# A gate matrix from bfloat16 one-hots: each token's product in three bfloat16 parts, in place of one fp32 product

## The chip, the cores and the metric

The kernel runs on one NeuronCore of one Trainium2 chip. The metric is device time in microseconds, the median of several executions. One further execution was taken with the hardware profiler; all rows below come from it.

## What is computed

The reference is one inference step of a one-layer decoder: mLSTM and retention heads, then a PEER mixer (product-key experts). Only the mixer's dense path matters here. For each token it picks 128 pairs (8 heads of 16) of expert and gate:

```python
top_s, top_pos = lax.top_k(cand_s, PEER_TOPK)          # per head: 16 of 256 candidates
e_idx = jnp.take_along_axis(cand_i, top_pos, axis=-1)  # expert = i1 * 128 + i2, of 16384
gate = jax.nn.softmax(top_s, axis=-1)
a = jax.nn.gelu(jnp.einsum('thkd,td->thk', u_tab[eb], xb).astype(jnp.float32), approximate=False)
return jnp.einsum('thk,thkd->td', (gb * a).astype(v_tab.dtype), v_tab[eb])
```

For 768 of the 1024 prompt tokens the kernel takes all 16384 experts, with a gate of zero where an expert wasn't picked. It therefore needs, for every token, the 128 x 128 matrix of gates, element (i2, i1) being the sum of the gates of the picks with that expert.

## The kernel before

The kernel is written in stages, each a block in which the engines run their own programs and meet by semaphores. `up_phase` holds four: the top-k stage, the decode stage, the gate stage and a stage that gathers rows for the other 256 tokens. In all four PE also works through the 128 units `e` of the dense up projection: a tile of `peer_u` is loaded (`u_load`), split into a high part by ScalarE (`u_high`) and a low part by DVE (`u_low`, L1070), and multiplied with the normalised tokens in two halves of 384 tokens (`u_unit`, 24 products of 384 columns each, L1081 to L1083). ScalarE applies the gelu (L1090) and SP stores it.

The decode stage (L1286 to L1396) turns the top-k results into three numbers for each pick: i1, i2 and the gate. PE transposes them, ScalarE writes them to `e3T` (L1349): 128 picks on the partitions, 3 x 776 values along each (768 dense tokens and 8 sample tokens). DVE's last operations there make `e_tok` and `gate_tok` for the 256 other tokens (L1394, L1395) and one `u_low` for each of nine token tiles.

The gate stage (L1399 to L1489) goes over the 768 dense tokens in 96 steps of STEP = 8. In each step DVE makes three tensors of 8 x 128 elements in fp32, by comparing `iota` (0 to 127) with a column of `e3T`: `raw` (where is i2; L1484), `one1[:, b]` (where is i1; L1485) and `one2[:, b]` = `raw` times the gate (L1487). `b` alternates, so there are two buffers. DVE waits for the step two before to leave PE (`step_done`) and, ahead of `raw`, for its own `one2` of the step before (`hot2`). PE waits for `hot1` and `hot2` and does one product for each token: `one2[:, b, k, :]` as the loaded operand, `one1[:, b, k, :]` as the moving one (L1438). The sum over the 128 picks is the token's gate matrix. Four tokens fill a PSUM bank; ScalarE copies each bank into `gbuf` (L1460). After every second step PE does one `u_unit`, after every fourth DVE does one `u_low`. 8 steps fill half of `gbuf`, which SP stores in one transfer of 4 MB (L1421), in its queue ahead of the next `u_load`. The stage after it reads `e3T` again, for the 8 sample tokens (L1601, L1643).

Of the kernel before, what the change touches and what calls it, by code (L numbers as in the profile page):

```python
# [13 lines left out]
BF16 = mybir.dt.bfloat16  # L14
I32 = mybir.dt.int32
ALU = mybir.AluOpType
# [3 lines left out]
P = 128  # L20
# [4 lines left out]
NS = 8  # L25
# [5 lines left out]
PH, NK, TOPK = 8, 128, 16  # L31
GROUPS = [range(0, 4), range(4, NC), range(NC, NT)]
SUB = 64
DENSE = 768
TG = DENSE // P
GT = NC - TG
NG = GT * P
NU = NG + NS
# [5 lines left out]
STEP = 8  # L44
# [992 lines left out]
def up_phase(nc, A, own, sb, ps, sem, ident, hn, x2_dram, hs_dram, g_dram, a_dram, ys, yt, idx, wt):  # L1037
# [4 lines left out]
    uh, ul = (sb(own, "u_" + x, [P, 2, ND, P], F32R) for x in ("hi", "lo"))  # L1042
    av = sb(own, "act_tile", [P, 2, DENSE])
    iota = sb(own, "iota", [P, NK])
    e3T = sb(own, "e3T", [P, 3, DENSE + NS])
    e_tok = sb(own, "e_tok", [P, GT, 2, NK])
    gate_tok = sb(own, "gate_tok", [P, NG])
    pu = [ps(own, f"u_p{g}") for g in range(2)]
    u_in, a_out = ([sem(f"{x}{i}") for i in range(2)] for x in ("u_in", "a_out"))
    uhi_done, ulo_done, up_done, gelu_done, iota_in = (  # L1050
# [2 lines left out]
    def u_load(sp, e, s, first=False):  # L1053
        if not first:
            sp.wait_ge(ulo_done, e - 1)
        sp.dma_start(u_raw[:, s], A["peer_ut"][e]).then_inc(u_in[s], 16)
# [11 lines left out]
    def u_low(dve, e, s):  # L1068
        dve.wait_ge(uhi_done, e + 1)
        nc.vector.tensor_tensor(ul[:, s], u_raw[:, s], uh[:, s].bitcast(F32), ALU.subtract).then_inc(ulo_done, 1)  # L1070
# [22 lines left out]
    with ExitStack() as both:  # L1093
# [192 lines left out]
        with ExitStack() as st, nc.Block() as block:  # L1286
# [6 lines left out]
            se = sb(st, "d_se", [P, NT, PH, TOPK])  # L1293
            sm = sb(st, "d_sum", [P, NT * PH, 2])
            gt = sb(st, "d_gate", [P, NT, K8])
            pt = [ps(st, f"d_t{i}") for i in range(2)]
            diff_done, exp_done, ident_done, oh_done, gt_done, t_done, t_out, chain = (
                sem(n) for n in ("d_diff", "d_exp", "d_ident", "d_oh_done", "d_gtdone", "d_tdone", "d_tout", "d_chain"))
# [2 lines left out]
            PET = TG + 1  # L1301
# [55 lines left out]
            def _(dve):  # L1357
# [16 lines left out]
                for i, t in enumerate(ORDER):  # L1374
# [20 lines left out]
                        v.tensor_copy(gate_tok[:, (t - TG) * NK:(t - TG + 1) * NK], gt[:, t, :])  # L1395
                    u_low(dve, E0 + i + 2, i % 2)  # L1396


    with ExitStack() as st, nc.Block() as block:  # L1399
        HALF = STEP // 2  # L1400
        NSTEP = SUB // STEP
        one1, one2 = (sb(st, f"one{i}", [P, 2, STEP, NK]) for i in (1, 2))
        raw = sb(st, "raw", [P, STEP, NK])
        gbuf = sb(st, "gbuf", [P, 2, NK, SUB])
        pg = [ps(st, f"g_p{i}") for i in range(4)]
        hot1, raw_done, hot2, step_done, bank_full, bank_out = (
            sem(n) for n in ("g_hot1", "g_raw", "g_hot2", "g_step", "g_full", "g_bank_out"))
        saved = [sem(f"g_saved{i}") for i in range(2)]

        @block.sync  # L1410
        def _(sp):
            for s in range(2):
                sp.sem_inc(saved[s], 16)
            with sp.Fori(0, NSUB // 2) as j:
                for s in range(2):
                    for p in range(2):
                        e = G0 + 4 * j + 2 * s + p
                        u_load(sp, e + 2, p)
                        a_store(sp, e, p)
                    sp.wait_ge(bank_out, (2 * NSTEP) * (2 * j + s + 1) + 4)  # L1420
                    sp.dma_start(g_dram[:, :, 2 * j + s].rearrange("q i e t -> i q e t"),  # L1421
                                 gbuf[:, s, :, :].rearrange("i (q e) t -> i q e t", e=2)).then_inc(saved[s], 16)
            for s in range(2):
                sp.wait_ge(saved[s], 16 * (NSUB // 2) + 16)

        @block.tensor
        def _(pe):
            pe.sem_inc(step_done, 2)
            with pe.Fori(0, NSUB // 2) as j:
                for s in range(2):  # L1430
                    for n in range(NSTEP):
                        i, b = (2 * j + s) * NSTEP + n, n % 2
                        pe.wait_ge(hot1, i + 1)
                        pe.wait_ge(hot2, i + 2)
                        for k in range(STEP):
                            if k % HALF == 0:
                                pe.wait_ge(bank_out, 2 * i + k // HALF + 1)
                            last = nc.tensor.matmul(pg[2 * b + k // HALF][:, (k % HALF) * NK:(k % HALF + 1) * NK],  # L1438
                                                    one2[:, b, k, :], one1[:, b, k, :], start=True, stop=True)
                            if k == HALF - 1:  # L1440
                                last.then_inc(bank_full, 1)
                        last.then_inc(step_done, 1)
                        if n % 2:
                            u_unit(pe, G0 + 4 * j + 2 * s + n // 4, n // 4, n // 2 % 2)

        @block.scalar
        def _(act):
            act.sem_inc(bank_out, 4)
            with act.Fori(0, NSUB // 2) as j:
                for s in range(2):  # L1450
                    act.wait_ge(saved[s], 16 * j + 16)
                    for n in range(NSTEP):
                        i, b = (2 * j + s) * NSTEP + n, n % 2
                        for c in range(2):
                            if c == 0:
                                act.wait_ge(bank_full, i + 1)
                            else:
                                act.wait_ge(step_done, i + 3)
                            t = n * STEP + c * HALF
                            nc.scalar.activation(gbuf[:, s, :, t:t + HALF],  # L1460
                                                 pg[2 * b + c][:, :].rearrange("p (t i) -> p i t", t=HALF),
                                                 ACT.Copy).then_inc(bank_out, 1)
                        if n % 2:
                            p, half = n // 4, G0 // 2 + 2 * j + s
                            e = G0 + 4 * j + 2 * s + p
                            u_gelu(act, e, p, n // 2 % 2, half)
                            if n // 2 % 2:
                                u_high(act, e + 2, p, half + 1)

        @block.vector  # L1470
        def _(dve):
            v = nc.vector
            dve.sem_inc(hot2, 1)
            dve.wait_ge(iota_in, 16)
            io = iota[:, :].unsqueeze(1).broadcast_to([P, STEP, NK])
            with dve.Fori(0, NSUB // 2) as j:
                for s in range(2):
                    for n in range(NSTEP):
                        i, b = (2 * j + s) * NSTEP + n, n % 2
                        col = [e3T[:, q, bass.ds(i * STEP, STEP)].unsqueeze(2).broadcast_to([P, STEP, NK])  # L1480
                               for q in range(3)]
                        dve.wait_ge(step_done, i + 1)
                        dve.wait_ge(hot2, i + 1)
                        v.tensor_tensor(raw[:, :, :], io, col[1], ALU.is_equal).then_inc(raw_done, 1)  # L1484
                        v.tensor_tensor(one1[:, b], io, col[0], ALU.is_equal).then_inc(hot1, 1)  # L1485
                        dve.wait_ge(raw_done, i + 1)
                        v.tensor_tensor(one2[:, b], raw[:, :, :], col[2], ALU.mult).then_inc(hot2, 1)  # L1487
                        if n % 4 == 3:
                            u_low(dve, G0 + 4 * j + 2 * s + n // 4 + 1, (n // 4 + 1) % 2)  # L1489


    with ExitStack() as st, nc.Block() as block:
# [3 lines left out]
        idx_f = sb(st, "s_idxf", [P, NU])  # L1496
# [99 lines left out]
        def _(dve):  # L1596
            v = nc.vector
            for t in range(GT):
                v.scalar_tensor_tensor(idx_f[:, t * NK:(t + 1) * NK], e_tok[:, t, 0, :], float(NK), e_tok[:, t, 1, :],
                                       ALU.mult, ALU.add).then_inc(idxf_done, 1)  # L1600
            v.scalar_tensor_tensor(idx_f[:, NG:NU], e3T[:, 0, DENSE:DENSE + NS], float(NK), e3T[:, 1, DENSE:DENSE + NS],  # L1601
                                   ALU.mult, ALU.add).then_inc(idxf_done, 1)
            dve.wait_ge(idxf_done, GT + 1)
            v.tensor_copy(idx[:, :], idx_f[:, :]).then_inc(idx_done, 1)  # L1604
# [25 lines left out]
            for j in range(J0, J1):  # L1630
                u_low(dve, 2 * j + 1, 1)
                if j == J0 + 1:
                    dve.wait_ge(hr_in, 16)
                if j == JG - 1:
                    dve.wait_ge(h_in, 16 * NS)
                rows_of(j, 0)
                if j < J1 - 1:
                    u_low(dve, 2 * j + 2, 0)
                rows_of(j, 1)
                if j == JG:  # L1640
                    dve.wait_ge(act_done, 1)
                    dve.wait_ge(zero_done, 1)
                    v.tensor_tensor(wd[:, :, :].rearrange("p a b -> p (a b)")[:, 0:NS * NS:NS + 1], dots[:, NG:NU],  # L1643
                                    e3T[:, 2, DENSE:DENSE + NS], ALU.mult).then_inc(wd_done, 1)
                    v.tensor_tensor(wt[:, :], dots[:, 0:NG], gate_tok[:, :], ALU.mult).then_inc(wt_done, 1)
                    dve.wait_ge(xt_in, 16)
                    dve.wait_ge(wt_done, 1)
# [355 lines left out]
```

## Time and profile before

| | |
|---|---|
| median of 3 runs | 3474.07 us (3472.54 to 3478.43) |
| the profiled execution's own time | 3476.1 us |
| its span, first to last instruction | 3474.3 us |
| PE, DVE, ScalarE, GpSimd busy | 95%, 73%, 29%, 21% |
| the gate stage in the span | some 1352 to 1738 us |

Times in a row are microseconds from the span's start or durations in microseconds, mean durations nanoseconds. PE is TensorE's matmuls, PEld its weight loads, which overlap them; DVE is VectorE, ACT ScalarE. Matmuls are pipelined: the duration of one is longer than its distance to the next, so rates are read from starts. An fp32 product is two passes, each with its own record.

### The profile page before, as it was taken

How to read it: one execution, taken by the hardware profiler on the slowest of the kernel's cores; microseconds unless marked ns; L12 is line 12 of the kernel's file. 1: busy time of each engine (PE TensorE's matmuls, PEld its weight loads, DVE VectorE, ACT ScalarE, POOL GpSimd, SP SyncE). 2: the span in 40 equal slices, each digit the busy share in tenths (PEclk: the TensorE clock that was granted, in tenths of full speed). 3: DMA queues.
4: the chain of work that ended last, by engine and by line, in shares of the span. 5: the costliest groups of instructions: out<-in, count | busy, mean ns of one | idle time of the engine just before them, and what ended most of it. 6: DMA issues, size and time to landing. Idle time of an engine off the chain costs nothing. (4 is left out here: it accounts for less than half of the span.)

```text
span 3474.3 us, 49500 instructions
## 1 busy us (share of the span) xinstructions
PE 3285.5 (95%) x17444; PEld 2896.5 (83%) x17444; DVE 2526.2 (73%) x5184; ACT 990.4 (29%) x1463; POOL 737.0 (21%) x565
## 2 busy tenths in 40 slices
PE   7989999797999899999989999998999999999998
PEld 5766777587999789999989999996888888888886
DVE  5465555434999968999847777765888887988884
ACT  3212322221111122444412222222333333333332
POOL 0000000000000000000046665554333333433320
PEclk9999999798999999999999999999999999999999
DMA  2111110222111122665599999997999999999983
GB/s 103 38 38 50 62 39 26 80 92 90 50 62 57 48 86 70 209 196 175 184 333 374 371 374 356 355 341 289 403 370 354 352 356 367 379 369 351 355 318 114
DMA packets 323132, 749.92 MB, mean 216 GB/s; under 512 B 22160, under 2 KB 153620, under 8 KB 321864
## 3 DMA queue, kind: packets, MB, share of 16 engines
q1 hardware_dynamic: 243240, 458.48, 36.8%
q0 software_dynamic: 79776, 290.00, 22.3%
q8 instruction: 60, 0.98, 0.1%
q14 instruction: 56, 0.46, 0.0%
HBM read 633.46 MB, written 114.94 MB: 215 GB/s over the span
## 5 line engine op out<-in xcount | busy, mean ns | idle before, releaser
L1081 PE MATMUL u_p<-hn_hi,u_hi 128*128 128x384 f32 x2048 | 705.3, 344 | 37.9 <-DVE u_lo L1070 19.8
L1082 PE MATMUL u_p<-hn_lo,u_hi 128*128 128x384 f32 x2048 | 697.6, 341 | 0.0
L1083 PE MATMUL u_p<-hn_hi,u_lo 128*128 128x384 f32 x2048 | 696.9, 340 | 0.0
L1514 POOL DMA_INDIRECT s_ring<-in_peer_u,row_idx x264 | 331.9, 1257 | 1332.0 <-DVE row_idx L1604 1109.1
L1759 PE MATMUL y_p<-v_hi,w_hi 128*128 128x512 f32 x1536 | 474.3, 390 | 19.5 <-DVE w_lo L1844 18.0
L1716 POOL DMA_INDIRECT y_ring<-in_peer_v,row_idx x240 | 355.9, 1483 | 618.1 <-DVE yt L1853 557.2
L1764 PE MATMUL y_p<-v_hi,w_lo 128*128 128x512 f32 x1536 | 473.4, 389 | 0.0
L1761 PE MATMUL y_p<-v_lo,w_hi 128*128 128x512 f32 x1536 | 473.3, 389 | 0.0
L1785 ACT ACTIVATE v_hi<-v_raw 128x1024 fp32r<-128x1024 f32 x256 | 257.2, 1052 | 664.5 <-PE y_p L1764 653.2
L1840 DVE TENSOR_TENSOR v_lo<-v_raw,v_hi 128x1024 fp32r<-128x1024 f32 x256 | 302.0, 1221 | 171.3 <-ACT v_hi L1785 171.3
L1081 PEld LDWEIGHTS u_p<-hn_hi,u_hi 128*128 128x128 f32 x2048 | 390.0, 190 | 42.6 <-issue 21.9
L1083 PEld LDWEIGHTS u_p<-hn_hi,u_lo 128*128 128x128 f32 x2048 | 389.9, 190 | 0.0
L1082 PEld LDWEIGHTS u_p<-hn_lo,u_hi 128*128 128x128 f32 x2048 | 389.8, 190 | 0.0
L1090 ACT ACTIVATE act_tile<-u_p 128x384 f32<-128x384 f32 x256 | 125.7, 491 | 920.2 <-PE u_p L1083 920.2
L1759 PEld LDWEIGHTS y_p<-v_hi,w_hi 128*128 128x128 f32 x1536 | 288.4, 188 | 81.1 <-DVE v_lo L1840 15.2
L1761 PEld LDWEIGHTS y_p<-v_lo,w_hi 128*128 128x128 f32 x1536 | 288.8, 188 | 60.1
L1764 PEld LDWEIGHTS y_p<-v_hi,w_lo 128*128 128x128 f32 x1536 | 288.6, 188 | 60.0
L1612 DVE CUSTOM_DVE_ANT_0 s_junk<-s_ring,s_hr 128x1024 f32<-128x1024 f32 x256 | 313.3, 1224 | 28.4 <-DVE s_dots L1612 1.0
L1853 DVE SCALAR_TENSOR_TENSOR yt<-y_ring,row_weight,yt 128x1024 f32<-128x1024 f32 x240 | 307.4, 1281 | 22.1 <-DMA y_ring<-in_peer_v,row_idx 5.2
L1070 DVE TENSOR_TENSOR u_lo<-u_raw,u_hi 128x1024 fp32r<-128x1024 f32 x128 | 156.1, 1220 | 185.3 <-ACT u_hi L1066 185.1
L324 PE MATMUL pp<-wp_hi,xn_hi 128*128 128x512 f32 (+1 forms) x576 | 247.5, 430 | 4.1 <-DVE wp_lo L583 3.7
L326 PE MATMUL pp<-wp_hi,xn_lo 128*128 128x512 f32 (+1 forms) x576 | 231.6, 402 | 0.0
(292 smaller groups left out, 4643.7 us busy)
## 6 DMA issues: line engine op xcount, KB each, us to landing
v_raw<-in_peer_v SPq DMA_DIRECT2D x128, 1024.0 KB, 7.0
u_raw<-in_peer_ut SPq DMA_DIRECT2D x128, 512.0 KB, 7.6
act_scratch<-act_tile SPq DMA_DIRECT2D x128, 384.0 KB, 5.4
gate_scratch<-gbuf SPq DMA_DIRECT2D x12, 4096.0 KB, 14.0
a_raw<-act_scratch SPq DMA_DIRECT2D x128, 384.0 KB, 7.6
g_raw<-gate_scratch SPq DMA_DIRECT2D x128, 384.0 KB, 9.2
wp_raw<-in_w_heads SPq DMA_DIRECT2D x64, 256.0 KB, 3.4
wq<-in_w_query SPq DMA_DIRECT2D x8, 1024.0 KB, 5.2
```

The lines of the kernel that those rows point to most:

```text
L1081: mm(b, uh[:, s, k, :], hn_hi[:, k, t], start=(k == 0), stop=False)
L1082: mm(b, uh[:, s, k, :], hn_lo[:, k, t], start=False, stop=False)
L1083: last = mm(b, ul[:, s, k, :], hn_hi[:, k, t], start=False, stop=(k == ND - 1))
L1514: nc.gpsimd.indirect_dma_start(out=ring[:, s, :], out_offset=None, in_=src, in_offset=bass.IndirectOffsetOnAxis(ap=idx[:, column:column + ...
L1612: v.tensor_tensor_reduce(junk[:, :], ring[:, n % RING, :], h, 1.0, 0.0, ALU.mult, ALU.add, dots[:, n:n + 1]).then_inc(dot_done, 1)
L1716: nc.gpsimd.indirect_dma_start(out=ring[:, n % RING, :], out_offset=None, in_=A["peer_v"], in_offset=bass.IndirectOffsetOnAxis(ap=idx[:, N ...
L1759: mm(py[t][i][:, :], wh[:, s, e, tok], vh[:, s, e, i * 512:(i + 1) * 512], start=a, stop=False)
L1761: mm(py[t][i][:, :], wh[:, s, e, tok], vl[:, s, e, i * 512:(i + 1) * 512], start=False, stop=False)
L1764: done = mm(py[t][i][:, :], wl[:, s, e, tok], vh[:, s, e, i * 512:(i + 1) * 512], start=False, stop=z)
L1785: ac(vh[:, s, e, :], v_raw[:, r, e, :], ACT.Copy).then_inc(vhi_done, 1)
L1840: v.tensor_tensor(vl[:, s, e, :], v_raw[:, r, e, :], vh[:, s, e, :].bitcast(F32), ALU.subtract).then_inc(vlo_done, 1)
L1853: v.scalar_tensor_tensor(yt[:, t, :], ring[:, n, :], wt[:, bass.ds(column, 1)], yt[:, t, :], ALU.mult, ALU.add).then_inc(add_done, 1)
```

## The change

The gate matrix is made from bfloat16 tensors. The gate is split into three bfloat16 parts whose sum is the fp32 value exactly. The plain one-hot is now that of i2 (`one2`, the loaded operand); the gate goes into `one1`, which has three parts, and PE adds three products for each token in PSUM. The tensors have the token innermost ([128 keys, 8 tokens] in place of [8 tokens, 128 keys]). `keys`, `iota` spread over 8 tokens in bfloat16, is made once. i1, i2 and the parts (`eb`, `gp`) are made by DVE at the end of the decode stage, behind its last `u_low`; `e3s` keeps the 8 sample tokens' values, and `e3T` lives only in the decode stage.

```diff
+                dve.wait_ge(t_out, PET)
+                ch.mark(v.tensor_copy(e3s[:, :, :], e3T[:, :, DENSE:DENSE + NS]))
+                ch.mark(v.tensor_copy(eb[:, :, :], e3T[:, 0:2, 0:DENSE]))
+                ch.link(v.tensor_copy(gp[:, 0, :], e3T[:, 2, 0:DENSE]))
+                ch.link(v.tensor_tensor(left[:, :], e3T[:, 2, 0:DENSE], gp[:, 0, :], ALU.subtract))
+                ch.link(v.tensor_copy(gp[:, 1, :], left[:, :]))
+                ch.link(v.tensor_tensor(left[:, :], left[:, :], gp[:, 1, :], ALU.subtract))
+                ch.link(v.tensor_copy(gp[:, 2, :], left[:, :]))
...
-        one1, one2 = (sb(st, f"one{i}", [P, 2, STEP, NK]) for i in (1, 2))
-        raw = sb(st, "raw", [P, STEP, NK])
+        one1 = sb(st, "one1", [P, 2, 3, NK, STEP], BF16)
+        one2 = sb(st, "one2", [P, 2, NK, STEP], BF16)
+        raw = sb(st, "raw", [P, NK, STEP], BF16)
+        keys = sb(st, "keys", [P, NK, STEP], BF16)
...
-                        pe.wait_ge(hot1, i + 1)
-                        pe.wait_ge(hot2, i + 2)
+                        pe.wait_ge(hot2, i + 1)
+                        pe.wait_ge(hot1, i + 2)
...
-                            last = nc.tensor.matmul(pg[2 * b + k // HALF][:, (k % HALF) * NK:(k % HALF + 1) * NK],
-                                                    one2[:, b, k, :], one1[:, b, k, :], start=True, stop=True)
+                            for q in range(3):
+                                last = nc.tensor.matmul(pg[2 * b + k // HALF][:, (k % HALF) * NK:(k % HALF + 1) * NK],
+                                                        one2[:, b, :, k], one1[:, b, q, :, k], start=(q == 0),
+                                                        stop=(q == 2))
...
-            io = iota[:, :].unsqueeze(1).broadcast_to([P, STEP, NK])
+            v.tensor_copy(keys[:, :, :], iota[:, :].unsqueeze(2).broadcast_to([P, NK, STEP])).then_inc(keys_done, 1)
+            dve.wait_ge(keys_done, 1)
...
-                        col = [e3T[:, q, bass.ds(i * STEP, STEP)].unsqueeze(2).broadcast_to([P, STEP, NK])
-                               for q in range(3)]
+                        t = bass.ds(i * STEP, STEP)
+                        e1, e2 = (eb[:, q, t].unsqueeze(1).broadcast_to([P, NK, STEP]) for q in range(2))
+                        part = gp[:, :, t].unsqueeze(2).broadcast_to([P, 3, NK, STEP])
                         dve.wait_ge(step_done, i + 1)
-                        dve.wait_ge(hot2, i + 1)
-                        v.tensor_tensor(raw[:, :, :], io, col[1], ALU.is_equal).then_inc(raw_done, 1)
-                        v.tensor_tensor(one1[:, b], io, col[0], ALU.is_equal).then_inc(hot1, 1)
+                        v.tensor_tensor(one2[:, b], keys[:, :, :], e2, ALU.is_equal).then_inc(hot2, 1)
+                        dve.wait_ge(hot1, i + 1)
+                        v.tensor_tensor(raw[:, :, :], keys[:, :, :], e1, ALU.is_equal).then_inc(raw_done, 1)
                         dve.wait_ge(raw_done, i + 1)
-                        v.tensor_tensor(one2[:, b], raw[:, :, :], col[2], ALU.mult).then_inc(hot2, 1)
+                        v.tensor_tensor(one1[:, b], raw[:, :, :].unsqueeze(1).broadcast_to([P, 3, NK, STEP]), part,
+                                        ALU.mult).then_inc(hot1, 1)
```

## Rows read from the trace of the kernel before

**Rows 1.** The page: busy time of each engine, and the chain that ended last.

```profile
PE 3285.5 (95%) x17444; PEld 2896.5 (83%) x17444; DVE 2526.2 (73%) x5184; ACT 990.4 (29%) x1463; POOL 737.0 (21%) x565
PE 29%; DMA 1%; SPq 0%; DVE 0%; issue 0%; ACT 0%; DVEq 0%; ACTq 0%
```

**Rows 2.** A stretch of the stage: length, busy PE to POOL, clock, DMA share, GB/s.

```profile
1450.00:1550.00 100.00, 99.76 (x709) 98.75 (x708) 94.91 (x83) 41.50 (x70) 0.00 (x0) 1.00 0.58 184
```

**Rows 3.** Groups of the stage: line, engine, operation, tiles, count | busy, mean ns | idle before.

```profile
L1484 DVE TENSOR_TENSOR raw<-iota,e3T 128x1024 f32<-128x1024 f32 x96 | 117.4, 1223 | 19.5 <-DVE one L1487 11.2 <-PE g_p L1438 7.5 <-PEq L1428 0.8
L1460 ACT ACTIVATE gbuf<-g_p 128x512 f32<-128x512 f32 x192 | 111.5, 595 | 53.8 <-PE g_p L1438 53.6
```

**Rows 4.** Waits inside the stage, 1365 to 1733: total us, times, longest us.

```profile
DVE raw L1484 <- DVE one L1487: 10.7, 47, 0.2
DVE raw L1484 <- PE g_p L1438: 7.2, 22, 0.5
ACT u_hi L1066 <- DMA u_raw<-in_peer_ut: 4.7, 11, 1.6
PEld g_p L1438 <- issue: 2.8, 11, 0.4
```

**Rows 5.** Timeline of PE: start us, duration us, engine, line, operation.

```profile
1361.76 0.42 PE L1081 MATMUL u_p<-hn_hi,u_hi 128*128 128x384 f32 x1
...
1503.83 0.19 PEld L1081 LDWEIGHTS u_p<-hn_hi,u_hi 128*128 128x128 f32 x1
...
1507.96 3.71 PEld L1438 LDWEIGHTS g_p<-one 128*128 128x128 f32 x32
...
1511.60 0.19 PEld L1081 LDWEIGHTS u_p<-hn_hi,u_hi 128*128 128x128 f32 x1
...
1732.82 0.42 PE L1081 MATMUL u_p<-hn_hi,u_hi 128*128 128x384 f32 x1
```

**Rows 6.** Timeline of DVE over four steps; in brackets the idle time before.

```profile
1502.31 1.23 DVE L1484 TENSOR_TENSOR raw<-iota,e3T 128x1024 f32<-128x1024 f32 x1 [0.39 <-PE g_p L1438]
1503.45 1.22 DVE L1485 TENSOR_TENSOR one<-iota,e3T 128x1024 f32<-128x1024 f32 x1
1504.59 1.22 DVE L1487 TENSOR_TENSOR one<-raw,e3T 128x1024 f32<-128x1024 f32 x1
1506.04 1.23 DVE L1484 TENSOR_TENSOR raw<-iota,e3T 128x1024 f32<-128x1024 f32 x1 [0.23 <-DVE one L1487]
...
1518.02 1.23 DVE L1484 TENSOR_TENSOR raw<-iota,e3T 128x1024 f32<-128x1024 f32 x1 [0.23 <-PE g_p L1438]
```

**Rows 7.** The decode stage's bfloat16 products: 32 loads in a row, and their group.

```profile
1268.79 1.79 PEld L1322 LDWEIGHTS d_t<-d_ident,d_oh 128*128 128x128 bf16 x32 [0.15 <-issue]
L1322 PEld LDWEIGHTS d_t<-d_ident,d_oh 128*128 128x128 bf16 x192 | 10.7, 98 | 0.9 <-issue 0.9
```

**Rows 8.** Groups of other stages on DVE and ACT, by size and layout.

```profile
L1835 DVE TENSOR_TENSOR wf<-a_raw,g_raw 128x384 f32<-128x384 f32 x256 | 130.6, 552 | 13.9 <-DMA g_raw<-gate_scratch 13.0
L1367 DVE CAST d_i<-ti 128x2304 f32<-128x2304 uint32 x1 | 1.4, 1352 | 0.0
L1388 DVE TENSOR_REDUCE d_sum<-d_se 128x72 f32<-128x1152 f32 x1 | 1.3, 1337 | 0.0
L1394 DVE TENSOR_REDUCE e_tok<-d_oh 128x256 f32<-128x4096 bf16 x2 | 14.9, 7442 | 0.1
L1197 ACT ACTIVATE qT<-s_q 128x344 f32<-128x344 f32 x48 | 22.0, 457 | 155.0 <-PE s_q L1164 155.0
```

**Rows 9.** Timeline between the decode stage and the gate stage.

```profile
1348.60 0.33 PE L1083 MATMUL u_p<-hn_hi,u_lo 128*128 128x384 f32 x1
...
1350.36 1.22 DVE L1070 TENSOR_TENSOR u_lo<-u_raw,u_hi 128x1024 fp32r<-128x1024 f32 x1
1352.39 1.23 DVE L1484 TENSOR_TENSOR raw<-iota,e3T 128x1024 f32<-128x1024 f32 x1 [0.82 <-PEq L1428]
...
1356.02 3.49 PEld L1438 LDWEIGHTS g_p<-one 128*128 128x128 f32 x16 [7.41 <-issue]
```

More of the change, by code:

```diff
@@ L1044, in up_phase @@
     iota = sb(own, "iota", [P, NK])
-    e3T = sb(own, "e3T", [P, 3, DENSE + NS])
+    e3s = sb(own, "e3s", [P, 3, NS])
     e_tok = sb(own, "e_tok", [P, GT, 2, NK])
     gate_tok = sb(own, "gate_tok", [P, NG])
+    eb = sb(own, "e_bf", [P, 2, DENSE], BF16)
+    gp = sb(own, "gate_parts", [P, 3, DENSE], BF16)
     pu = [ps(own, f"u_p{g}") for g in range(2)]
@@ L1295, in up_phase @@
             gt = sb(st, "d_gate", [P, NT, K8])
+            left = sb(st, "d_left", [P, DENSE])
+            e3T = sb(st, "e3T", [P, 3, DENSE + NS])
             pt = [ps(st, f"d_t{i}") for i in range(2)]
@@ L1401, in up_phase @@
         NSTEP = SUB // STEP
-        one1, one2 = (sb(st, f"one{i}", [P, 2, STEP, NK]) for i in (1, 2))
-        raw = sb(st, "raw", [P, STEP, NK])
+        one1 = sb(st, "one1", [P, 2, 3, NK, STEP], BF16)
+        one2 = sb(st, "one2", [P, 2, NK, STEP], BF16)
+        raw = sb(st, "raw", [P, NK, STEP], BF16)
+        keys = sb(st, "keys", [P, NK, STEP], BF16)
         gbuf = sb(st, "gbuf", [P, 2, NK, SUB])
         pg = [ps(st, f"g_p{i}") for i in range(4)]
-        hot1, raw_done, hot2, step_done, bank_full, bank_out = (
-            sem(n) for n in ("g_hot1", "g_raw", "g_hot2", "g_step", "g_full", "g_bank_out"))
+        keys_done, hot1, raw_done, hot2, step_done, bank_full, bank_out = (
+            sem(n) for n in ("g_keys", "g_hot1", "g_raw", "g_hot2", "g_step", "g_full", "g_bank_out"))
         saved = [sem(f"g_saved{i}") for i in range(2)]
@@ L1472, in _ @@
             v = nc.vector
-            dve.sem_inc(hot2, 1)
+            dve.sem_inc(hot1, 1)
             dve.wait_ge(iota_in, 16)
-            io = iota[:, :].unsqueeze(1).broadcast_to([P, STEP, NK])
+            v.tensor_copy(keys[:, :, :], iota[:, :].unsqueeze(2).broadcast_to([P, NK, STEP])).then_inc(keys_done, 1)
+            dve.wait_ge(keys_done, 1)
             with dve.Fori(0, NSUB // 2) as j:
@@ L1600, in _ @@
                                        ALU.mult, ALU.add).then_inc(idxf_done, 1)
-            v.scalar_tensor_tensor(idx_f[:, NG:NU], e3T[:, 0, DENSE:DENSE + NS], float(NK), e3T[:, 1, DENSE:DENSE + NS],
+            v.scalar_tensor_tensor(idx_f[:, NG:NU], e3s[:, 0, :], float(NK), e3s[:, 1, :],
                                    ALU.mult, ALU.add).then_inc(idxf_done, 1)
@@ L1643, in _ @@
                     v.tensor_tensor(wd[:, :, :].rearrange("p a b -> p (a b)")[:, 0:NS * NS:NS + 1], dots[:, NG:NU],
-                                    e3T[:, 2, DENSE:DENSE + NS], ALU.mult).then_inc(wd_done, 1)
+                                    e3s[:, 2, :], ALU.mult).then_inc(wd_done, 1)
                     v.tensor_tensor(wt[:, :], dots[:, 0:NG], gate_tok[:, :], ALU.mult).then_inc(wt_done, 1)
```

## The prediction

> **What bounds the kernel now.** I read the page first. TensorE (PE) is busy for 95% of the span, and the chain that ended last, nearly all PE, covers 30% of it from the end, so it doesn't reach back to the gate stage [rows 1]. The stage therefore has to be read by itself, and the table by stretch comes next: between 1450 and 1550 us PE shows 99.8 of 100 us busy and VectorE (DVE) 94.9, at a full granted clock (1.00) [rows 2]. So two engines are nearly full, and a change has to be costed on both.
>
> The timeline gives the true rates, because a busy PE is pipelined. The unit of the stage is a pair of steps (16 tokens) and one `u_unit` of 24 products. The first `u_unit` begins at 1361.76 and the last at 1732.82: 371.06 us for 47 pairs, 7.90 us each [rows 5]. There are 48 pairs. PE's own need in a pair: the `u_unit` from 1503.83 to 1507.96 takes 4.13 us, the 16 fp32 products from there to 1511.60 take 3.64 us. That is 32 passes, 0.114 us each (the trace shows two per fp32 product); together 7.77 us [rows 5].
>
> DVE's need: its three operations of 1024 elements take 1.22 us each [rows 3] and follow each other in 1.14 us, but `raw` sits 0.23 us idle behind the end of `one2`, so that one step is 3.73 us. One `u_lo` (1.22 us, 1.14 to the next) comes every four steps and takes the place of such a wait. Four steps run from `raw` at 1502.31 to `raw` at 1518.02, 15.71 us, or 7.86 us a pair [rows 6]. The waits agree: `raw` waits 47 times for DVE's own `one2` and 22 times for PE, PE's loads only 2.8 us in all [rows 4]. DVE sets the pace with PE 0.1 us behind it. Shortening DVE's part alone would bring 0.1 us a pair, PE's alone less.
>
> **The change, part by part.** *DVE in the loop.* `one2` and `raw` stay at 1024 elements, the product becomes 3072, all bfloat16. No row of before shows a two-input DVE operation on 16-bit data, so it is bounded. One end is one element per cycle: the operations of 384 and 1024 elements (0.552 and 1.223 us [rows 3, 8]) give 1.05 ns an element and 0.15 us fixed. The other is two: the cast of 2304 elements in 1.352 us [rows 8], so 0.52 ns. I take 0.52, because two bfloat16 inputs bring as many bytes per element (4) as that cast reads, where two fp32 inputs bring 8. Then 1024 elements take 0.69 us and 3072 take 1.75 us. With 0.08 us overlap to the next operation and 0.23 us where one waits for the one before it (`raw` to `one1` only, now), a step is 0.61 + 0.92 + 1.67 = 3.20 us. Four and a `u_lo` (1.14) are 13.94 us, 6.97 us a pair.
>
> The Trainium skill ("VectorE: DVE Perf Modes", the perf-mode tier table) gives `tensor_tensor` on bfloat16 in SBUF twice its fp32 rate. No run here shows it yet; by it the time would be the same.
>
> *PE in the loop.* 16 fp32 products of two passes go, 48 bfloat16 ones come. The nearest row is the decode stage's bfloat16 products of the same size, 32 of them back to back: 1.79 us for the loads, of which the last takes 0.098, so 1.69 / 31 = 0.055 us each; I use 0.056 [rows 7]. 48 make 2.69 us, with the `u_unit` 6.82 us a pair. But those operands lie side by side. Here the token is innermost, so each column of `one2[:, b, :, k]` and of `one1[:, b, q, :, k]` lies 8 bfloat16 (16 bytes) from the last, and no row shows PE reading such an operand. The low bound is 0.056. For the high one there is DVE's reduction over `d_oh`, which steps 512 bytes at each element: 4096 in 7.44 us, 1.78 ns each, against 1.03 ns side by side (1152 in 1.337 us) [rows 8]. As a ratio (1.73) that makes 0.097 us a product, as a time 128 x 1.78 ns = 0.228 us. On the other side, the evacuation L1460 steps 512 bytes through PSUM at every element and pays nothing: 512 elements in 595 ns and 344 side by side in 457 ns [rows 3, 8] are 0.82 ns an element. One row speaks for each; I take 0.056, as the only row of this engine with this type, and keep both ends.
>
> The page "Advanced Engine Details and Errata" of the Trainium skill (SBUF Cachelines) speaks against this change: lines have 16 bytes, and two accesses to a line are needed to hide the memory's latency. The DVE reduction agrees with it, and no row shows PE under it.
>
> *Together.* DVE needs 6.97 us, PE 6.82. With two buffers DVE starts a step only after PE has ended the step two before; today this costs 7.90 - 7.86, and I allow as much: 7.00 us. Gain: (7.90 - 7.00) x 48 = 43 us.
>
> *Cover of the rest.* ScalarE's evacuations keep their shape: 4 x 0.6 + 0.49, and 1.05 every other pair, is under 3.5 us of 7. Its `u_hi` already waits for the `u_raw` load, up to 1.6 us [rows 4]. With two pairs 1.8 us shorter it waits up to 3.4; the next evacuation that PE needs is two steps and a `u_unit` (6.8 us) away, so this is hidden. Without that cover it would cost 12 x 1.8 = 22 us. DMA moves 184 GB/s in the stage at a share of 0.58 [rows 2] and has room.
>
> *Ahead of the loop, on the path.* The new DVE operations stand behind the last `u_lo` of the decode stage. DVE is what that junction waits for: PE's last product begins at 1348.60, the `u_lo` at 1350.36 ends at 1351.58, the first `raw` starts at 1352.39, PE's first gate product at 1356.02 [rows 9]. Nothing hides them. `e3s` 0.09, `eb` (1536 at 0.52 ns) 0.87, three `gp` copies 0.55 + 0.23 each, two subtractions (768 at 1.05 ns) 0.96 + 0.23 each: 5.7 us. `keys` 0.69 + 0.23 = 0.9 us more; the first step is 0.25 us shorter. Sum +6.4 us. Bounds: 9 with every copy at one element a cycle, 5.5 if the 0.8 us before the first `raw` absorbs a part. Behind the 7.1 us idle PE's first 16 loads already run at half pace (3.49 us, where 32 later take 3.71 [rows 5, 9]); a longer idle brings no new state, at worst one more step at that pace, 1.3 us. The index and weight operations of the next stage only read `e3s` instead of `e3T`: nothing.
>
> Sum: -43 + 6.4 = -36.6 us. The profiled execution took 3476.1 us (span 3474.3 and 1.8 around it), 2.0 above the median of 3474.07, so the same difference from the median gives 3437.5 us.
>
> **The rivals.** (1) *PE pays for the spaced columns*, and becomes the bound where DVE was. It decides from (7.90 - 0.13 - 4.13) / 48 = 0.076 us a product, where 0.13 is the 6.4 us spread over the pairs. At 0.097 us a pair is 4.13 + 4.66 = 8.79 us: +43 + 6.4, 3523 us. At 0.114, the pace of an fp32 pass, it is 9.60: +82 + 6.4, 3562 us. For it: the DVE reduction and the 16-byte step. Against: ScalarE's free steps, in PSUM. (2) The same with the time per element and not the ratio: 0.228 us, 15.07 us a pair, +344 + 6.4, 3825 us. (3) *The change does not do what it says on DVE*: one element a cycle. A step is 1.14 + 1.45 + 3.29 = 5.88, a pair 12.33 us: +213 + 6.4, 3693 us. Against it: the bytes, and that single-input operations here do run at two. (4) A small PE price, 0.073 to 0.079 us: it takes the gain and ends within 0.2% of before.
>
> By the Trainium skill's rule on SBUF cachelines ("Advanced Engine Details and Errata") rival 1 or 2 would come true; with one access to a line where two are wanted, it lies nearest to rival 1.
>
> **How the numbers follow.** Forecast 0.45 (own range 3428 to 3450: from PE's 6.82 us a pair with 5.5 us ahead of the loop, to 7.2 with 9); rival 1 0.26; rival 2 0.12; rival 3 0.08; rival 4 0.05; another small loss or gain 0.04, split. The range must reach rival 1 and leaves out rivals 2 and 3 (0.20 in all): 3428 to 3565. Beyond 0.2% (7 us), about what a measurement of this kernel can tell from none: faster 0.45 + 0.02 = 0.47, within 0.06, slower 0.26 + 0.12 + 0.08 + 0.01 = 0.47. The likeliest single case is faster, yet the slower ones together weigh as much: it hangs on one unseen price.
>
> **What would show it.** In the profile after: 24 products of a step in 1.35 us (right), 2.3 to 2.7 (rival 1), 5.5 (rival 2). DVE's 1024-element operation at 0.69 us and the 3072 one at 1.75 (right), or 1.22 and 3.37 (rival 3). If right, DVE still waits for its own `raw` and PE for `one1`; under rival 1 DVE sits idle behind PE's steps and PE shows no gap. The idle of PE ahead of the stage grows from 7.1 to some 13.5 us. Wrong would be, above all, the 0.056.

## The result, and the profile after

The kernel became slower: 3919.91 us (median, 3916.68 to 3928.18) against 3476.25 us, a ratio of 1.1267 with an interval of 1.1244 to 1.1291. The prediction, 3437.5 us in a range of 3428 to 3565, was wrong in sign and in size. The profiled execution has a span of 3914.9 us, 440.6 us more than before.

Nearly all of it (439.6 us) is in the gate stage: from PE's first gate product to the last product of the last `u_unit` it now lasts from 1357.42 to 2177.90 us, where it lasted from 1356.02 to 1736.94. One stretch of it, with the columns of [rows 2]:

```profile
1450.00:1550.00 100.00, 100.00 (x423) 75.37 (x422) 40.04 (x39) 19.91 (x33) 0.00 (x0) 0.70 0.22 70
```

PE is still busy for the whole stretch, but with 423 records where [rows 2] has 709, DVE's busy time fell from 94.9 to 40.0 us, and the granted clock from 1.00 to 0.70. PE alone is the bound now. The groups of the stage, to be read against [rows 3] and [rows 7] (the product is now L1454, `one2` L1502, `raw` L1504, `one1` L1506, the evacuation L1477, the first product of a `u_unit` L1083):

```profile
L1454 PE MATMUL g_p<-one 128*128 128x128 bf16 x2304 | 548.1, 414 | 12.3 <-DVE one L1506 12.3
L1454 PEld LDWEIGHTS g_p<-one 128*128 128x128 bf16 x2304 | 331.5, 146 | 213.0 <-issue 19.9
L1083 PE MATMUL u_p<-hn_hi,u_hi 128*128 128x384 f32 x384 | 173.2, 451 | 0.0
L1506 DVE TENSOR_TENSOR one<-raw,gate_parts 128x3072 bf16<-128x3072 bf16 x96 | 168.8, 1759 | 11.9
L1502 DVE TENSOR_TENSOR one<-keys,e_bf 128x1024 bf16<-128x1024 bf16 x95 | 65.8, 693 | 473.7 <-PE g_p L1454 473.7
L1504 DVE TENSOR_TENSOR raw<-keys,e_bf 128x1024 bf16<-128x1024 bf16 x95 | 65.1, 685 | 0.0
```

DVE does what was forecast: 0.69 us for 1024 elements and 1.76 for 3072, so (1759 - 693) / 2048 = 0.52 ns an element, half of fp32's 1.05. But `one2` now waits 473.7 us in all for PE, where `raw` waited 7.2 [rows 4]. PE's timeline over a pair:

```profile
1512.44 11.43 PE L1454 MATMUL g_p<-one 128*128 128x128 bf16 x48
1523.51 0.68 PE L1083 MATMUL u_p<-hn_hi,u_hi 128*128 128x384 f32 x1
1524.63 0.52 PE L1083 MATMUL u_p<-hn_hi,u_hi 128*128 128x384 f32 x1
1525.59 0.52 PE L1083 MATMUL u_p<-hn_hi,u_hi 128*128 128x384 f32 x1
1526.55 0.52 PE L1083 MATMUL u_p<-hn_hi,u_hi 128*128 128x384 f32 x1
1527.43 0.34 PE L1083 MATMUL u_p<-hn_hi,u_hi 128*128 128x384 f32 x1
...
1529.53 0.66 PE L1454 MATMUL g_p<-one 128*128 128x128 bf16 x2
```

[rows 5] have a pair of before by the starts of PE's loads. These are the same pair's products, so that both are read alike:

```profile
1503.86 0.42 PE L1081 MATMUL u_p<-hn_hi,u_hi 128*128 128x384 f32 x1
...
1508.13 3.73 PE L1438 MATMUL g_p<-one 128*128 128x128 f32 x32
1511.62 0.42 PE L1081 MATMUL u_p<-hn_hi,u_hi 128*128 128x384 f32 x1
```

Two things are new. The 48 products take 11.07 us (1512.44 to 1523.51), 0.231 us each, four times the 0.056 of [rows 7]; the gate products of before took 3.49 us in all. And the `u_unit` behind them takes 6.02 us (1523.51 to 1529.53) where it took 4.27 (1503.86 to 1508.13): its first half runs at 0.96 us for three products, its end at 0.53, as before. A pair is 17.09 us, not 7.90. The clock says why for the `u_unit`. These are stretches of that run of products, PE's and PEld's busy time of L1454 alone, then the clock:

```profile
1512.60:1515.60 3.00, 3.00 (x14) 1.88 (x14) 1.00 0.00 0
1515.60:1518.60 3.00, 3.00 (x15) 1.84 (x14) 0.74 0.00 0
1518.60:1521.60 3.00, 3.00 (x15) 1.85 (x14) 0.50 0.00 0
```

Inside this run of gate products the granted clock goes from 1.00 to 0.50 (2.4 to 1.2 GHz), and so it does in 47 of the 48 runs; the first one begins at 0.50. The products themselves don't notice: 14 or 15 in 3 us at either level. The `u_unit` that follows pays, until the clock is back.

The junction ahead of the loop came out near its forecast: PE's first gate product stands behind 12.28 us of idle time, 5.2 more than the 7.1 between the two PE times of [rows 9].

```profile
1357.42 0.89 PE L1454 MATMUL g_p<-one 128*128 128x128 bf16 x3 [12.28 <-DVE one L1506]
```

So 48 x (17.09 - 7.90) = 441 us stands beside 440.6 of span. Of it, 48 x (11.07 - 3.49) = 364 is from the products and 48 x (6.02 - 4.27) = 84 from the clock behind them; 48 x (7.90 - 3.49 - 4.27) = 7 goes off for PE's waits in the old pace. The 5.2 us ahead of the loop hardly show in the span: in this execution PE begins its last product before the junction at 1344.82, in [rows 9] at 1348.60.

### The profile page after: what moved, and what is told of

Same layout as the page of the kernel before. It is cut to its first block and busy times, and to the rows that moved or that the text cites. A ratio compares the mean times of both kernels' runs of the same rounds, so it can differ in the third digit from the quotient of the medians.

```text
span 3914.9 us, 50949 instructions
## 1 busy us (share of the span) xinstructions
PE 3722.5 (95%) x18212; PEld 3133.5 (80%) x18212; DVE 2491.2 (64%) x5192; ACT 995.0 (25%) x1463; POOL 745.5 (19%) x565
## 5 line engine op out<-in xcount | busy, mean ns | idle before, releaser
L1083 PE MATMUL u_p<-hn_hi,u_hi 128*128 128x384 f32 x2048 | 745.4, 364 | 37.7 <-DVE u_lo L1072 19.6
L1084 PE MATMUL u_p<-hn_lo,u_hi 128*128 128x384 f32 x2048 | 733.5, 358 | 0.0
L1085 PE MATMUL u_p<-hn_hi,u_lo 128*128 128x384 f32 x2048 | 726.9, 355 | 0.0
L1454 PE MATMUL g_p<-one 128*128 128x128 bf16 x2304 | 548.1, 414 | 12.3 <-DVE one L1506 12.3
L1454 PEld LDWEIGHTS g_p<-one 128*128 128x128 bf16 x2304 | 331.5, 146 | 213.0 <-issue 19.9
L1083 PEld LDWEIGHTS u_p<-hn_hi,u_hi 128*128 128x128 f32 x2048 | 419.4, 205 | 46.6 <-issue 21.9
L1085 PEld LDWEIGHTS u_p<-hn_hi,u_lo 128*128 128x128 f32 x2048 | 417.6, 204 | 0.0
L1084 PEld LDWEIGHTS u_p<-hn_lo,u_hi 128*128 128x128 f32 x2048 | 417.1, 204 | 0.0
L1502 DVE TENSOR_TENSOR one<-keys,e_bf 128x1024 bf16<-128x1024 bf16 x96 | 66.5, 693 | 474.0 <-PE g_p L1454 473.7
```

Source lines behind the costliest of these rows:

```text
L1083: mm(b, uh[:, s, k, :], hn_hi[:, k, t], start=(k == 0), stop=False)
L1084: mm(b, uh[:, s, k, :], hn_lo[:, k, t], start=False, stop=False)
L1085: last = mm(b, ul[:, s, k, :], hn_hi[:, k, t], start=False, stop=(k == ND - 1))
```

## The experiments

The theory after the result: a column of PE's operand that lies 16 bytes from the last costs 1.8 ns, and the clock falls within such a run. The rivals: the three accumulating products hinder each other; it is the loaded operand; the clock is a matter of its own.

**Both operands side by side.** Only PE's addresses change.

```diff
-  one2[:, b, :, k], one1[:, b, q, :, k], start=(q == 0), stop=(q == 2)
+  one2[:, b, :, :].rearrange("p n s -> p (n s)")[:, k * NK:(k + 1) * NK],
+  one1[:, b, q, :, :].rearrange("p n s -> p (n s)")[:, k * NK:(k + 1) * NK], start=(q == 0), stop=(q == 2)
```

> The changed kernel with PE reading 128 columns that lie side by side in both operands; the buffers, DVE's work and every wait are as they were (the products thus read other columns, so the gate matrix isn't the one wanted). Theory A, the spaced columns are the cost: a product falls from 0.231 us to 0.056, a pair of steps with its u_unit from 17.1 us to 7.0 with DVE as the bound, the granted clock goes back to 1.00 in the stage, and the time is some 3440 us. Theory B, the three accumulating products into one place of PSUM hold each other up, whatever their operands: still 0.23 us a product and 3920 us. Theory C, the spacing costs, but the lower clock is a thing of its own: 0.056 a product, the u_unit still at 6.0 us, some 8.9 us a pair and 3530 us.

Measured: 3438.63 us against 3482.37 for the kernel before, measured beside it, a ratio of 0.9892 (0.9849 to 0.9936). Its stretch (columns as in [rows 2]), PE's timeline and its waits:

```profile
1450.00:1550.00 100.00, 100.00 (x1045) 97.42 (x1042) 93.67 (x94) 46.51 (x81) 0.00 (x0) 1.00 0.68 219
```

```profile
1483.83 2.85 PE L1454 MATMUL g_p<-one 128*128 128x128 bf16 x48
1486.49 0.43 PE L1083 MATMUL u_p<-hn_hi,u_hi 128*128 128x384 f32 x1
...
1490.77 2.85 PE L1454 MATMUL g_p<-one 128*128 128x128 bf16 x48
```

```profile
ACT u_hi L1068 <- DMA u_raw<-in_peer_ut: 24.9, 11, 3.3
DVE one L1503 <- PE g_p L1454: 9.5, 23, 0.7
```

The products take 2.66 us, 0.055 each, a pair 6.94 us (1483.83 to 1490.77), the clock is 1.00. Theory B is out: three accumulating products cost what three products cost. So is C: the clock comes back with the addresses. `u_hi` waits for its load up to 3.3 us, as the prediction had it (3.4), and PE doesn't feel it. One thing is not as expected: PE sets the pace now, with 2.66 us of products and 4.28 of `u_unit`. From 1365 us on DVE waits for PE 23 times, PE not once for DVE.

**One operand at a time.** The same edit for the moving operand alone, so that only the loaded one is spaced (first), and for the loaded one alone (second).

> As e_none, but the loaded operand one2 has its columns 16 bytes apart again; the moving operand one1 is read side by side. If the cost is in the load: 0.23 us a product and some 3920 us. If it is in the moving stream: 0.056 to 0.08 us a product (the load may grow from 0.098 to 0.146 us and stay hidden behind the moving stream), 7.0 to 8.0 us a pair, 3440 to 3490 us.

> As e_none, but the moving operand one1 has its columns 16 bytes apart again; the loaded operand one2 is read side by side. If the cost is in the moving stream: 0.23 us a product, a u_unit of 6.0 us behind each run of them, some 3920 us. If it is in the load: 0.056 us and 3440 us. If each of the two costs a part: both this and the run with the loaded operand spaced lie between.

Measured, one execution each: 3448.65 us with the loaded operand spaced, 3919.11 us with the moving one. The first kernel's timeline and group, then the second kernel's timeline:

```profile
1484.25 3.16 PE L1454 MATMUL g_p<-one 128*128 128x128 bf16 x48
1487.22 0.42 PE L1083 MATMUL u_p<-hn_hi,u_hi 128*128 128x384 f32 x1
...
L1454 PEld LDWEIGHTS g_p<-one 128*128 128x128 bf16 x2284 | 146.0, 147 | 7.8 <-issue 7.8
```

```profile
1480.34 11.05 PE L1454 MATMUL g_p<-one 128*128 128x128 bf16 x48
1491.03 0.68 PE L1083 MATMUL u_p<-hn_hi,u_hi 128*128 128x384 f32 x1
...
1497.41 2.88 PE L1454 MATMUL g_p<-one 128*128 128x128 bf16 x12
```

With the loaded operand spaced a load lasts 147 ns in place of 98, and a product takes 0.062 us (2.97 / 48): 48 x (2.97 - 2.66) = 15 us over the stage. With the moving operand spaced a product takes 0.223 us (10.69 / 48), the `u_unit` behind them 6.38 us and a pair 17.07: the whole loss is there.

**The moving operand's step.** Columns 1 to 16 bfloat16 apart, one step width for each of the eight steps, each on its own line.

```diff
+  mv = one1[:, b, :, :, :].rearrange("p q n s -> p (q n s)")
+  if n == 0: nc.tensor.matmul(out, w, mv[:, k:k + 1 * (NK - 1) + 1:1], **f)
...
+  elif n == 7: nc.tensor.matmul(out, w, mv[:, k:k + 16 * (NK - 1) + 1:16], **f)
```

> As e_none, but the moving operand's columns lie 1, 2, 3, 4, 6, 8, 12 and 16 bfloat16 apart in steps 0 to 7 of each eight (the loaded operand side by side; the gate matrix isn't the one wanted). Theory of pieces of 16 bytes, each 1.8 ns: the product's time follows the number of pieces that its 128 columns touch: 0.056 at 1 and 2 (16 and 32 pieces), some 0.09 at 3, 0.115 at 4, 0.17 at 6, and 0.23 at 8, 12 and 16 alike. Theory of any gap: 0.23 from 2 on. Theory of distance: it keeps rising past 8. Steps come in pairs, so the stage's own time (some 12 us a pair on average by the first theory) says little; it is the time of a product by line that counts.

The time was 3676.15 us (one execution). PE's timeline over eight steps (L1459, L1461, ... are steps 1, 2, 3, 4, 6, 8, 12, 16; L1083 is the start of the `u_unit` behind each pair):

```profile
1603.05 1.52 PE L1459 MATMUL g_p<-one 128*128 128x128 bf16 x24
1604.41 1.58 PE L1461 MATMUL g_p<-one 128*128 128x128 bf16 x24
1605.80 0.42 PE L1083 MATMUL u_p<-hn_hi,u_hi 128*128 128x384 f32 x1
...
1610.09 2.28 PE L1463 MATMUL g_p<-one 128*128 128x128 bf16 x24
1612.20 2.97 PE L1465 MATMUL g_p<-one 128*128 128x128 bf16 x24
1614.92 0.43 PE L1083 MATMUL u_p<-hn_hi,u_hi 128*128 128x384 f32 x1
...
1619.23 4.29 PE L1467 MATMUL g_p<-one 128*128 128x128 bf16 x24
1623.34 5.62 PE L1469 MATMUL g_p<-one 128*128 128x128 bf16 x24
1628.61 0.68 PE L1083 MATMUL u_p<-hn_hi,u_hi 128*128 128x384 f32 x1
...
1634.15 5.62 PE L1471 MATMUL g_p<-one 128*128 128x128 bf16 x24
1639.59 5.75 PE L1473 MATMUL g_p<-one 128*128 128x128 bf16 x24
1644.97 0.68 PE L1083 MATMUL u_p<-hn_hi,u_hi 128*128 128x384 f32 x1
```

From start to start, by 24; a piece is 16 bytes of the moving operand's row:

| step in bfloat16 | 1 | 2 | 3 | 4 | 6 | 8 | 12 | 16 |
|---|---|---|---|---|---|---|---|---|
| 16-byte pieces touched | 16 | 32 | 48 | 64 | 96 | 128 | 128 | 128 |
| us for a product | 0.057 | 0.058 | 0.088 | 0.113 | 0.171 | 0.220 | 0.227 | 0.224 |

From 48 pieces on, a product takes 1.72 to 1.83 ns for each piece, and no more beyond 8. That is the first theory; any gap costing the same, and distance, are both out. At a step of one the 128 columns themselves are the limit (16 pieces would take 0.028 us); at two their time and that of 32 pieces (0.056 us) are about the same.

The same lines show behind which runs the clock is low. The `u_unit` behind steps 3 and 4 begins with a product of 0.43 us, at a granted clock of 1.00 (1614.92 to 1619.20); those behind 6 and 8 and behind 12 and 16 begin with 0.68 us, at 0.54 (1628.61 to 1631.60) and 0.50 (1644.97 to 1648.00).

**Two tokens innermost: a version that keeps the gain.** If a step of two is free for PE, DVE needs only its rows of two. The gate's parts and DVE's operations are laid out to match (not shown).

```diff
-  one1 = sb(st, "one1", [P, 2, 3, NK, STEP], BF16)
-  one2 = sb(st, "one2", [P, 2, NK, STEP], BF16)
+  one1 = sb(st, "one1", [P, 2, STEP // 2, 3, NK, 2], BF16)
+  one2 = sb(st, "one2", [P, 2, STEP // 2, NK, 2], BF16)
...
-  one2[:, b, :, k], one1[:, b, q, :, k]
+  one2[:, b, k // 2, :, k % 2], one1[:, b, k // 2, q, :, k % 2]
```

> The whole change, with two tokens innermost in place of eight: the tensors are [4, 128, 2] (one1 [4, 3, 128, 2]), the gate's parts lie as [384, 3, 2], so that every column of a product is 4 bytes from the last and DVE's rows are two bfloat16 long. The piece theory (a moving column costs by the 16-byte pieces it touches): 0.058 us a product as in the step of two, PE 6.95 us a pair, DVE 6.97, some 3440 us, 1.0% faster than before. If DVE wants longer rows for two elements per cycle: 1.22 and 3.37 us for its operations, 12.3 us a pair and some 3690 us. If the loaded operand, too, pays by its step and isn't hidden: some 0.07 us a product and 3460 us.

Measured: 3440.27 us against 3482.43, a ratio of 0.9888 (0.9868 to 0.9908): 1.1% faster than before, 12% faster than the change as it was made. Its stretch, PE's timeline and DVE's:

```profile
1450.00:1550.00 100.00, 100.00 (x1033) 97.50 (x1031) 92.62 (x93) 43.64 (x77) 0.00 (x0) 1.00 0.73 235
```

```profile
1504.84 3.05 PE L1454 MATMUL g_p<-one 128*128 128x128 bf16 x48
...
1511.97 2.92 PE L1454 MATMUL g_p<-one 128*128 128x128 bf16 x48
...
1518.98 2.94 PE L1454 MATMUL g_p<-one 128*128 128x128 bf16 x48
```

```profile
1506.54 0.69 DVE L1503 TENSOR_TENSOR one<-keys,e_bf 128x1024 bf16<-128x1024 bf16 x1 [0.34 <-PE g_p L1454]
1507.15 0.69 DVE L1505 TENSOR_TENSOR raw<-keys,e_bf 128x1024 bf16<-128x1024 bf16 x1
1507.99 1.76 DVE L1507 TENSOR_TENSOR one<-raw,gate_parts 128x3072 bf16<-128x3072 bf16 x1 [0.15 <-DVE raw L1505]
1509.67 0.68 DVE L1503 TENSOR_TENSOR one<-keys,e_bf 128x1024 bf16<-128x1024 bf16 x1
```

A pair takes 7.13 and 7.01 us, DVE's step is 3.13 us from `one2` to `one2` (forecast 3.20), its rows of two run as fast as rows of eight, and the clock stays at 1.00.

**Does the clock fall because the runs are long?** The spaced layout again, but each `u_unit` is cut in halves behind each step (first), or its 24 products are spread behind each token's three (second).

```diff
-  if n % 2:
-      u_unit(pe, e, n // 4, n // 2 % 2)
+  u_some(pe, e, n // 4, n // 2 % 2, 12 * (n % 2), 12 * (n % 2) + 12)                           # halves
+  u_some(..., 12 * (n % 2) + 3 * k // 2, 12 * (n % 2) + 3 * (k + 1) // 2)                      # spread, for each k
```

> The changed kernel as it is (columns 16 bytes apart), with each u_unit cut in two halves of 12 products, one behind each step of 24 spaced products, so that the runs of spaced products last 5.5 us in place of 11. All of it is computed. Theory K1, the clock falls inside long runs of spaced products: it stays nearer to 1.00, 12 products of the u_unit take 2.1 us, a pair 15.2 us, some 3830 us. K2, the mix over a pair decides: the granted clock stays at 0.70, 17.1 us a pair and 3920 us. K3, it now never recovers between the runs: 0.32 us for each product of a u_unit, 18.8 us a pair, some 4000 us.

> The changed kernel with the 24 products of each u_unit spread among the 48 spaced ones (one or two behind each token's three). All of it is computed. K1: no run of spaced products is longer than 0.7 us, the clock stays at 1.00, 15.2 us a pair, some 3830 us. K2: clock 0.70, 17.1 us, 3920 us. K3: the lower level throughout, 18.8 us a pair, some 4000 us.

In the diff, `e` stands for the unit's number. Measured, one execution each: 3996.3 us in halves, 4017.43 us spread, both slower than the long runs. A stretch of the halves and one of the spread (columns as in [rows 2]):

```profile
1450.00:1550.00 100.00, 100.00 (x394) 75.57 (x394) 36.19 (x36) 17.51 (x29) 0.00 (x0) 0.74 0.27 85
```

```profile
1450.00:1550.00 100.00, 100.00 (x379) 66.50 (x377) 34.25 (x34) 16.92 (x28) 0.00 (x0) 0.50 0.24 76
```

Spread, the clock never leaves 0.50: K3, with 4000 us forecast for it. In halves no theory fits whole. The mean clock is no lower than with long runs (0.74 against 0.70), yet the time is K3's: the clock's high part now lies mostly over the spaced products, which gain nothing by it (0.81 from 1495.40 to 1500.83), and 12 products of the `u_unit` mostly run at 0.32 us each (0.50 from 1500.83 to 1504.84):

```profile
1500.83 0.69 PE L1097 MATMUL u_p<-hn_hi,u_hi 128*128 128x384 f32 x1
1501.31 0.53 PE L1097 MATMUL u_p<-hn_lo,u_hi 128*128 128x384 f32 x1
1501.63 0.53 PE L1097 MATMUL u_p<-hn_hi,u_lo 128*128 128x384 f32 x1
...
1504.84 5.81 PE L1467 MATMUL g_p<-one 128*128 128x128 bf16 x24
```

So the length of a run isn't what lowers the clock; shorter runs leave less of the `u_unit` at the high level. K1 and K2 fall.

## Why the prediction was wrong

- *The bound before* (DVE first, PE 0.1 us behind): nothing contradicts it. With PE's operands side by side both come down together, to 6.94 us a pair (forecast 7.00), but in the other order: PE needs 6.94 for a forecast of 6.82 and DVE waits for it.
- *DVE in the loop* was right: 0.69 and 1.76 us for 0.69 and 1.75, a step of 3.13 for 3.20.
- *Ahead of the loop* was near: 5.2 us for 6.4, just below its bounds of 5.5 to 9.
- *The cover* was right: `u_hi` waits up to 3.3 us, for a forecast of 3.4, at no cost.
- *PE in the loop* is the step that failed: "I take 0.056, as the only row of this engine with this type". It is 0.231 us, the other end that was written beside it (0.228, rival 2, chance 0.12, left out of the range). With 0.056 in place, the same sum gave 3437.5 us, and the kernel with side-by-side operands took 3438.63. That the two are 1 us apart is partly luck: beside a kernel before of 3482.37 us the gain was 43.7 us (22 to 53), for a forecast of 36.6.
- *The size of rival 2* was short too: 3825 us for 3919.91. The missing term is in the main the clock, 84 us, which none of the cases had: a `u_unit` was costed at 4.13 us everywhere.

The rows at hand allowed a better choice. The row of bfloat16 products [rows 7] had the right engine and type but not the layout, and the layout was what was new. The evacuation [rows 3, 8] had the layout, but reads PSUM. Only DVE's reduction [rows 8] had both layout and memory, and its 1.78 ns an element is what PE paid as well, within 2%. Its step is 512 bytes; the widest that PE was measured with is 32. That both prices have one cause is likely by this agreement, not shown. The prediction carried it over as a ratio too (0.097 us, rival 1, with twice the chance of rival 2). A ratio to an engine's own pace means nothing if the price is the memory's: PE at 2.4 GHz loses four times, DVE 1.73 times, for the same nanoseconds. The `u_unit` fitted this price too: 384 fp32 columns are 96 pieces of 16 bytes, and 4.13 us / 24 = 0.172 us for them is 1.79 ns a piece. It doesn't prove it, since 0.448 ns a column is also near the 0.43 of [rows 7]; but no row showed any engine taking pieces faster than that.

The Trainium skill's rule ("Advanced Engine Details and Errata", SBUF Cachelines: 16-byte lines, at least two hits on a line to absorb the memory's latency) spoke against the change and was right in kind. On how many hits are enough the runs differ from it, and they decide: two bfloat16 columns to a line (step 4) still cost double, 0.113 us; four (step 2) are free, 0.058.

That the clock's fall came from the spaced products is shown by the side-by-side run (1.00) and by the kernel with two tokens innermost, whose products are the wanted ones (1.00). What in them lowers it was not taken apart.

## What to carry to other kernels

Where a layout is turned so that one engine gets dense rows, cost every other engine that reads it, by a row with the same memory and spacing, and carry such a price over in nanoseconds, not as a ratio. For PE's moving operand in bfloat16, keep the columns within 4 bytes of each other; DVE's dense rows need be no longer than two, so both fit. When a product becomes slow at an unchanged count of columns, also look at the granted clock of the dense work next to it.

## What the runs showed of the hardware

- PE's moving operand in bfloat16 costs about 1.76 ns for each 16-byte piece that it touches (from 48 pieces for 128 columns on), at a granted clock of 1.00 and 0.50 alike (14 or 15 products in 3 us); a busy PE at 100% of a stretch says nothing of it.
- The loaded operand with columns 16 bytes apart is nearly free: 147 for 98 ns a load, 0.062 for 0.055 us a product.
- Within runs of products with a step of 16 bytes the granted clock goes from 1.00 to 0.50 with PE busy all the time; with such products spread among dense ones it stays at 0.50 throughout the stretch. Behind runs with a step of 3 or 4 bfloat16 it was still 1.00.
- DVE's two-input operation on bfloat16 takes 0.52 ns an element also with rows of two elements and one operand repeated: 0.69 us for 1024, 1.76 for 3072.
